# Gate rows ahead of the output projection's weights, a fill spread over all of attention, and expert weights that no longer wait for the token gathers

## The reference

```python
mod  = silu(c) @ w_ada[i] + b_ada[i]        # 6 vectors of 1024: shift, scale, gate for attention, the same for the experts
modc = silu(c_ctx) @ w_ada[i] + b_ada[i]    # the same for the 256 context tokens
h  = rmsnorm(x, g_attn[i]) * (1 + sc_a) + sh_a
q, k, v = h @ w_qkv[i]                      # 16 heads of 64, 4 key heads
o  = attention(...)                         # layer 0 windowed with a sink, layer 1 global; both also over the context
x  = x + gt_a * (o @ w_o[i])
hf = rmsnorm(x, g_ffn[i]) * (1 + sc_f) + sh_f
y  = hier_moe(hf)                           # group, then 2 of 8 experts in it; each: (silu(xe @ w_gate) * (xe @ w_up)) @ w_down
x  = x + gt_f * y
```

## Time and profile before

| | |
|---|---|
| median of 3 runs | 2276.75 us (2274.09 to 2280.97) |
| the profiled execution's own time | 2274.09 us |
| its span | 2272.2 us |
| TensorE busy | 1934.4 us, 85% |
| VectorE, ScalarE, GpSimd busy | 618.9, 375.9, 136.6 us |
| mean granted TensorE clock | 0.958 |
| read from DRAM | 597 MB, 278 GB/s over the span |
| chain that ended last | TensorE 59%, DMA 32% |

### The profile page before, as it was taken

One profiled execution on the slowest core, in us unless ns is written; L12 is line 12 of the kernel. 1 busy time (PEld: TensorE's weight loads), 2 busy tenths in 40 slices (PEclk: granted clock), 3 DMA queues, 4 the chain that ended last, 5 costly groups with the idle time before them and its releaser, 6 DMA issues.

```text
span 2272.2 us, 19872 instructions
## 1 busy us (share of the span) xinstructions
PE 1934.4 (85%) x7977; PEld 895.8 (39%) x7977; DVE 618.9 (27%) x1372; ACT 375.9 (17%) x791; POOL 136.6 (6%) x184
## 2 busy tenths in 40 slices
PE   4999997878787877998877777777699999899998
PEld 1444553333333332454333333232345554445553
DVE  1234555000000003664300000000363332262332
ACT  1123511000000001251100000000212230212220
POOL 1000001000000002000100000000100000100000
PEclk9999998999999898999899999998799999999999
DMA  9733408999999998533799999996733334534331
GB/s 341 302 141 120 177 28 340 425 427 427 426 423 425 421 421 334 196 131 123 312 426 427 426 427 424 419 420 251 270 126 111 121 111 148 183 106 147 111 112 56
DMA packets 121679, 611.46 MB, mean 269 GB/s; under 512 B 13156, under 2 KB 15476, under 8 KB 96364
## 3 DMA queue, kind: packets, MB, share of 16 engines
q1 hardware_dynamic: 104128, 572.52, 62.3%
q0 software_dynamic: 17168, 36.56, 4.8%
q10 hardware_dynamic: 288, 1.05, 0.1%
HBM read 597.43 MB, written 33.62 MB: 278 GB/s over the span
## 4 chain that ended last, share of the span: by engine, by line
PE 59%; DMA 32%; DVE 5%; issue 1%; SPq 1%; ACT 1%; POOL 0%; POOLq 0%; DVEq 0%
DMA ring<-in_w_up 30%; PE bank L938 12%; PE bank L718 12%; PE bank L798 6%; PE bank L952 5%; PE bank L1016 4%; PE bank L552 3%; PE bank L1168 2%; PE bank L859 2%; PE bank L672 2%; PE bank L648 1%; PE bank L537 1%; DMA ring<-in_w_ada 1%; PE bank L625 1%; PE bank L659 1%
## 5 line engine op out<-in xcount | busy, mean ns | idle before, releaser
L718 PE MATMUL bank<-ring,big 128*64 128x512 f32 x3072 | 717.8, 621 | 202.0 <-DMA ring<-in_w_gate 85.9
L718 PEld LDWEIGHTS bank<-ring,big 128*64 128x64 f32 x3072 | 256.8, 143 | 638.2 <-issue 597.6
L938 PE MATMUL bank<-ring,big 128*128 128x512 f32 (+1 forms) x640 | 282.2, 590 | 0.0
L2022 DVE TENSOR_TENSOR big<-big,bank 128x512 f32<-128x512 f32 x32 | 22.0, 687 | 615.6 <-PE bank L718 615.6
L938 PEld LDWEIGHTS bank<-ring,big 128*128 128x128 f32 x640 | 117.5, 190 | 126.2 <-issue 126.1
L798 PE MATMUL bank<-ring,big 128*128 128x512 f32 x320 | 139.5, 594 | 0.0
L552 PE MATMUL bank<-ring,small 128*2 128x512 f32 x192 | 94.4, 637 | 31.9 <-DMA ring<-in_w_ada 31.9
L952 PE MATMUL bank<-ring,big 128*128 128x512 f32 x256 | 115.7, 611 | 1.7 <-issue 1.7
L1186 ACT ACTIVATE big<-bank 128x512 f32<-128x512 f32 (+1 forms) x86 | 48.2, 575 | 351.5 <-PE bank L798 101.5
L553 PE MATMUL bank<-ring,small 128*2 128x512 f32 x192 | 94.4, 637 | 0.0
L2028 DVE COPY big<-bank 128x512 f32<-128x512 f32 x32 | 22.1, 691 | 259.1 <-PE bank L718 259.1
(11 more groups left out here) (371 smaller groups left out, 1771.8 us busy)
## 6 DMA issues: line engine op xcount, KB each, us to landing
ring<-in_w_gate SPq DMA_DIRECT2D x64, 2048.0 KB, 18.3
ring<-in_w_up SPq DMA_DIRECT2D x64, 2048.0 KB, 19.4
ring<-in_w_down SPq DMA_DIRECT2D x64, 2048.0 KB, 19.0
ring<-in_w_in SPq DMA_DIRECT2D x26, 2048.0 KB, 7.6
ring<-in_w_ada SPq DMA_DIRECT2D x24, 2048.0 KB, 18.3
ring<-in_w_qkv SPq DMA_DIRECT2D x6, 2048.0 KB, 20.0
y_d<-big SPq DMA_DIRECT2D x1, 12288.0 KB, 44.1
ring<-in_w_branch SPq DMA_DIRECT2D x6, 2048.0 KB, 7.6
```

The costliest lines, as they stand in the source:

```text
L718: ins = nc.tensor.matmul(bank[half * CAP:(half + 1) * CAP, :], lhs[:, k, half * CAP:(half + 1) * CAP], w[:, k * step + c0:k * step + c0 + ...
L938: ins = nc.tensor.matmul(u[:, 0:cols], HT2[:, k, tile * P:(tile + 1) * P], w[:, 0:KD * cols].rearrange("p (k n) -> p k n", k=KD)[:, k, :], ...
```

## The change

There are three edits. In the list, `rows` stands ahead of the two chunks of `w_o`, in both layers; the slots of these three change with it. The fill's 32 items are dealt over all 27 steps of layer 0's attention, where they were dealt two by two over the first 16. SP no longer waits for the first two gathers before the first `w_down`.

```diff
+            put(("rows", layer), mod_d[layer, 0:LAT if layer == 0 else 1, 3 * D:5 * D])
             for c in range(2):
                 put(("wo", layer, c), kmajor(t["w_o"][layer], c * 512, 512))
-            put(("rows", layer), mod_d[layer, 0:LAT if layer == 0 else 1, 3 * D:5 * D])
...
             items = [(p, k) for p in range(2, 6) for k in range(KD)]
-            steps = 2 * len(UNITS[0]) // 3
-            return [items[len(items) * i // steps:len(items) * (i + 1) // steps] for i in range(len(UNITS[0]) + 3)]
+            steps = len(UNITS[0]) + 3
+            return [items[len(items) * i // steps:len(items) * (i + 1) // steps] for i in range(steps)]
...
                 if before_in_slot[n] is not None:
                     sp.wait_ge(*last_use[before_in_slot[n]])
-                if stream[n][0] in [("moe", layer, 0, 2, 0) for layer in range(2)]:
-                    for s_gathered in expert_sems[stream[n][0][1]][1]:
-                        sp.wait_ge(s_gathered, 16)
                 sp.dma_start(dst, src).then_inc(w_in[slot], 16)
```

## The result

The changed kernel takes 2312.93 us in the median (2311.96 to 2314.50) against 2275.42 before on the same chip: a ratio of 1.0162, 95% interval 1.0142 to 1.0181, which is 36.9 us more (the two medians lie 37.5 us apart). The forecast was 24.6 us more, 2301, with 2311 as the upper end. The direction and the places were right; four of the five terms were too small. The profiled execution has a span of 2311.7 us, 39.5 above the one before, which was one of the faster executions of its kernel.

The account below looks back on a forecast made before the run. The prediction took DMA engines to bound the expert stretches and TensorE layer 0's attention. Its terms, 17.2 + 1.9 + 2.1 + 2.0 + 1.4 = 24.6 us, on 2276.75 gave 2301 us, range 2290 to 2311.

Parts of the forecast that it names:

- The fill spread over all 27 steps: Layer 0's attention: fill items cover late TensorE pauses at no cost in TensorE time; gain 2.4 us, bounds 0 and 3.
- The gate rows ahead of w_o: Layer 0's output projection waits for w_o 0, landing at 293.2 behind the rows: +17.2 us; layer 1 nothing.
- The clock: Layer 0's projection: the 17 us pause before it lowers TensorE's clock, +1.9 us, bounds 0 and 4.
- The slots turn: Layer 0 before routing: ada 1 c3 takes the rows' slot and lands late, +2.1 us, bounds 1.3 and 5.
- The wait for the gathers, removed: Start of both expert stages: w_down in flight slows the first gathers, partly won back; +2.0 us layer 0, +1.4 layer 1.
- Rival 1: Same 19.1 us stall at layer 0's projection, but the expert stages' gathers hardly suffer: 2296 us, chance 0.2.
- Rival 3: Expert stages: four w_down chunks leave the DMA-bound stream, 19.8 us against 19.1, so not slower: 2276 us, chance 0.05.
- Rival 2: More of everything: layer 1's gather +7.5, c3 5 us late, clock 4; 33 us in all, 2309 us, chance 0.14.

Follow-up runs that it names:

- the first edit alone: Kernel before with only the gate rows issued ahead of w_o, fill in 16 steps and wait for the gathers kept: 2283.0 us, ratio 1.0028.
- the third edit alone: Kernel before with only SP's wait for the first two gathers before the first w_down removed: 2284.3 us, ratio 1.0031.

## Why the prediction missed, point by point

**The fill spread over all 27 steps** was forecast at -2.4 inside attention; it gave -1.6 (-0.2 against a start of +1.4). The pauses in front of L659, 2.4 us in all, are gone as forecast: no row of L659 in the changed kernel's attention has one. But TensorE's busy time there rose from 125.6 to 126.4 us. The item before a change back to attention's own matmuls takes 0.53 us to the next start where 0.43 is the rule (239.95 to 240.48 and 239.53 to 239.95), and there are ten more such changes now; that makes 1.0 us by estimate, which no run tested. "The cost in TensorE time is nothing" was thus wrong by 0.8 us. The prediction also left out what the epilogue then waits for: with w_o in place it would have been Pool's gates (13.64 us of VectorE's idle time with the fill alone). In the changed kernel the stall covers that.

**The gate rows ahead of w_o** was forecast at +17.2 together with the fill and measured at 23.9 from the start of attention. This is the main step that failed. Its parts were right: 3.97 against 3.9 us to the issue, 15.2 against 15.54 for w_o 0, 21.2 against 20.5 for w_o 1. Wrong was "the sixteen records on the first chunk keep TensorE busy for 6.9: no second stall". The code fetches both chunks, and waits for both, ahead of the loop over tiles. The 5.5 us between the landings stand in full in the stall. With the wait moved they go, in the trace by 5.5 us, and the sentence would have been right for that kernel. In layer 1 the same order cost nothing, as forecast: the projection there starts 36.1 us later, as attention 1 does.

This step alone doesn't explain the size of the miss: with the prediction's own 21.2 for w_o 1 in place of 15.2 its sum would have been 2307. The stall was 6.7 us longer than forecast, c3 4.4 and the gathers 3.3, the clock 1.3 less; together 13.1 us, about what is missing between 24.6 and the 36.9 to 37.5 measured.

**The clock** was forecast at +1.9; the projection took 0.6 us more in all, within the bounds.

```profile
301.28 23.17 PE L859 MATMUL bank<-ring,big 128*128 128x512 f32 x48 [25.43 <-issue]
```

Its first 48 records took 23.17 us at a granted clock of 0.90, where they took 20.87 at 1.00: 2.3 us more after a pause of 25 us, and 1.6 and 2.4 in the two other runs with the stall. Of these, 1.7 came back by the end, 0.8 of it in the last eight records (5.38 us, 6.17 before). That part isn't told from chance: in the traces without a stall or a late gate the projection took 66.8 us once, 68.5 twice and 70.2 three times, and nearly all of the difference lies in its last rows.

**The slots turn** was forecast at +2.1 with bounds 1.3 and 5; it is +6.5 in the trace and +6.4 as the whole of the first edit alone. The mechanism was right, c3 in the rows' slot, and so was the path through L877. The size was wrong: 8.6 us for its landing were taken from the rows' own load, which ran beside 1 MB of Pool's. c3 needed 12.7 in the changed kernel and 13.1 with the first edit alone; 3.3 of these are Pool's two gate vectors, 0.9 the loads behind it. The remaining 1 us over the 7.8 of an undisturbed load was not separated; the h_d store is still beside it there. The rows were a poor measure for it: with the attention gates loaded earlier they landed in 7.5 us, so that the same megabyte cost them 1.1 us and c3 3.3. Why it differs no run showed.

**The wait for the gathers, removed**: forecast +2.0 and +1.4, measured +3.4 and +3.3. The gathers' company cost 3.1 us in layer 0 (2.9 forecast) and 6.7 in layer 1, near the upper bound of 7.5 where 4.4 was taken. What comes back was 3.4 in layer 1 (3.0 forecast), and in layer 0 none by the start of attention 1 (0.9 forecast). The third edit alone gives 7 us; its absence among three 6.6, with wide intervals.

**The rivals.** Rival 1, gathers that hardly suffer, falls by the third edit alone. Rival 3 falls too: no microsecond left the stream. Rival 2, more of everything, was nearest in total (2309). It was right in part, with c3 at 5 us and layer 1's gather at 7.5, but it had the stall at 17.2 and the clock at 4. The stall's own bounds, 10.6 to 20.2, left out the 23.9 because they came from the landing of one load (8.6) and the median of a pair (18.2), not from the second chunk's 21.2.

## What to carry to other kernels

When a load is put behind one that must wait, count until the last operand that the consumer's code asks for has landed, and read in the code where those waits stand: in a trace in which everything came early, they leave no row. Two edits that cost little alone (6.4 and 2.5 us here) can meet: together they cost 21 us more than their sum. And a wait that looks like idle time on a queue can be what gives a small transfer, for which everything waits, the engines to itself: here it was worth 7 us to hold 8 MB back.

## What the runs showed that was not expected

A 0.5 MB indirect gather that took 3.3 us on idle DMA engines took some 10 to 11 us beside weight loads of 2 MB, in the changed kernel, with the third edit alone and with the wait for w_o 1 moved. A 2 MB load at the head of SP's queue took 7.8 us alone, some 10 beside one 0.5 MB store with four loads behind it, and 12.2 to 13.1 with 1 MB of GpSimd's loads added. The profile gave no cause ("issue") for a pause in which TensorE waited for two loads in turn, the last of them not the one read first: 5.53 us here, which only the landing times explained. With the second wait moved, the same row names the load.
